# A streaming hybrid layer on one core: idle products in the norm gaps, a turn back through eight banks, a router that holds its weights, and queries projected last

## The chip, the cores and the metric

The kernel runs on one core of one Trainium2 chip. The metric is the device time in microseconds of one execution, from launch to end; lower is better. The profile is of one execution, and its span (first to last instruction) is a little shorter than its time. The engines are TensorE (PE in the rows; PEld is its weight load), VectorE (DVE), ScalarE (ACT), GpSimd (POOL) and SyncE (SP), which issues most transfers. L544 is line 544 of the kernel.

## The reference

One inference step of two layers, D = 1024, in float32, over 256 new prompt tokens and 32 sample tokens (T = 288 columns in all). Each layer:

```
z = x @ w_in, columns = [rnn stream | q | k | v | rnn gate | attn gate]
branch A: causal depthwise conv (width 4) -> RG-LRU (per-token linear recurrence)
branch B: rotary GQA over a chunk-banded sliding window with per-head sinks
m = sigmoid(g_rnn) * (A @ w_br_rnn) + sigmoid(g_attn) * (B @ w_br_attn)
x = LayerNorm(alpha * x + m @ w_out)
scores = sigmoid(x @ w_router); 8 of 64 experts by group-limited top-k of scores + e_bias
x = LayerNorm(alpha * x + shared_expert(x) + sum over the 8 of gate_e * expert_e(x))
```

There are 16 query heads and 2 key/value heads of 64; each expert is silu(x w1) * (x w3), then w2, with a hidden width of 256.

## The kernel before, in words

Activations stand feature-major in xT, eight chunks of 128 features by 288 tokens. The matrices of a layer, apart from the experts', are read in 33 pieces (PIECES) through a ring of three slots. SyncE asks for a piece when the piece three places earlier has been used. Work between engines is ordered by hand with semaphores.

**Projections.** over_features (L518) makes one chunk of output: eight products with a 128x128 weight and 288 moving columns; a float32 product shows as two records. The order is eight chunks of the recurrent stream, eight of Q, one of K, then V (L594). They go by turns into PSUM banks 0 and 1: item i uses bank i % 2, and bank_of waits until every earlier item of that bank has been evicted (z_free). ScalarE evicts the stream and V. VectorE runs the convolution (L1268, L1271), in layer 0 then decay_rates and sink_tables (small tables of parameters), and then the rotation of Q and K (L1287 to L1293), which reads the bank. The gate products of the recurrence (L602) follow, again by turns in banks 0 and 1, evicted by ScalarE with a sigmoid. Then come attention, the gates, the branch merge and w_out. VectorE's next work behind the last rotation is k_rows (L1297).

**Norms, two in each layer.** to_tokens turns the sum from feature-major to token-major: 24 turns (L552) into banks 2 to 7. VectorE takes statistics (L1226 and on), and ScalarE writes the normalised rows to tok (L936). When all are written, fill_xT turns them back (L544): for each of eight feature chunks, two turns of 128 rows and one of 32 into bank c % 2. ScalarE evicts the even chunks and VectorE the odd ones (norm_back, L944 and L1251), with gain and bias, into xT. TensorE waits at L544 for the rows, with nothing to do.

**Router, behind the first norm.** For each of three token tiles TensorE takes eight products with xT as stationary operand and 64 columns of w_router moving (L728); logits land token-major in bank 2. Then come shared_up(0) (16 products, L518), the rank products (L743 to L746) that wait for sel_ready, shared_up(1), and the first gather (L778 to L781). Meanwhile ScalarE rounds tok to a short format (xh, L1055) and VectorE makes the rest (xl, L1431), three tiles each. Then ScalarE takes the sigmoid of the logits (L1059), and VectorE runs the routing chain, L1441 to L1469 for the choice (sel_ready), to L1477 for the gate, then rank and the one-hot matrices.

**Experts.** A round is 16 turns of four experts, 15 of them in a hardware loop: up (L793), turn, down (L813), combine (L834, L835), gather. After the round TensorE loads the number of rounds from memory (L871), branches over the further rounds, which aren't needed here, and goes on to the second norm. The last layer ends with to_tokens(xT) and the store.

Of the kernel before, what the change touches and what calls it, by code (L numbers as in the profile page):

```python
# [53 lines left out]
SWAP = (0, 1, 5, 6)  # L54
QUAD = 4
# [24 lines left out]
Z_RNN, Z_Q, Z_K, Z_V, Z_LRU, Z_GATE, Z_OUT, Z_FILL1, Z_SH2, Z_FILL2, Z_N = 0, 8, 16, 17, 18, 34, 50, 58, 66, 74, 82  # L80
# [4 lines left out]
PIECES = ([("in", 256 * j) for j in range(4)] + [("q", j) for j in range(4)] + [("in", K_OFF)]  # L85
# [4 lines left out]
D_IN, D_Q, D_KV, D_G, D_BR, D_OUT, D_ROUTER = 0, 4, 8, 9, 17, 25, 29  # L90
# [25 lines left out]
def piece_landed(L, d):  # L116

    return L * SLOT_INC[d % RING] + sum(16 * DMAS.get(PIECES[x][0], 1) for x in range(d % RING, d + 1, RING))

# [6 lines left out]
def build(nc, inp, out, depth, alpha):  # L126
    with ExitStack() as ctx:
# [102 lines left out]
        s2.close()  # L230
        raw = B1f[:, 0:2 * depth * P].rearrange("p (k l c) -> p k l c", k=2, l=depth)
# [77 lines left out]
        xl_ready = sem("xl_ready")  # L309
        logits = sem("logits")  # L310
# [32 lines left out]
        def wait_piece_used(eng, L, d):  # L343

            kind, at = PIECES[d]
            if d < D_Q:
                i = Z_RNN + 2 * d + 1
            elif d < D_KV:
                i = Z_Q + 2 * (d - D_Q) + 1
            elif d == D_KV:  # L350
                i = Z_V
            elif d < D_BR:
# [4 lines left out]
            elif d < D_ROUTER:  # L357
                i = Z_OUT + 2 * (d - D_OUT) + 1
            elif kind == "router":
                eng.wait_ge(logits, L + 1)  # L360
# [145 lines left out]
        def _(pe):  # L506
            mm, transpose = nc.tensor.matmul, nc.tensor.transpose

            def bank_of(L, i):

                pe.wait_ge(z_free[i % 2], z_count(L, i))
                return ps[:, i % 2, :]
# [41 lines left out]

            for s in (w13_done, w2_done, c_full, ohT_full, hid_turned, xg_full):
                pe.sem_inc(s, FREE)
# [3 lines left out]
            fill_xT(lambda c: pe.wait_ge(z_free[c % 2], c // 2) if c >= 2 else None)  # L560
# [11 lines left out]
            for L in range(depth):  # L572
# [10 lines left out]
                for c in range(KC):  # L583
                    if c % 2 == 0:
                        piece(L, D_Q + c // 2)
                    over_features(bank_of(L, Z_Q + c), D_Q + c // 2, c % 2 * P, xk, T).then_inc(z_ready[c % 2], 1)

# [7 lines left out]
                last.then_inc(z_ready[Z_V % 2], 1)  # L595

# [119 lines left out]
                to_tokens(yP)  # L716
                pe.wait_ge(tok_act, (2 * L + 1) * NT)
# [150 lines left out]
                round_of(pe.snap(done), meanwhile=shared_down)  # L868
                pe.wait_ge(rounds_set, L + 1)
# [8 lines left out]
                to_tokens(ffT)  # L878
                pe.wait_ge(tok_act, (2 * L + 2) * NT)
# [10 lines left out]
        def _(act):  # L890
# [13 lines left out]
            def z_item(L, i):  # L904
                act.wait_ge(z_ready[i % 2], z_count(L, i) + 1)
                return ps[:, i % 2, :]
# [742 lines left out]
```

## Time and profile before

| | |
|---|---|
| time, median of 3 runs | 1719.76 us (1717.3 to 1720.46) |
| profiled execution, its own time | 1717.09 us |
| its span | 1715.3 us |
| TensorE busy | 1640.0 us, 96% |
| VectorE busy | 719.6 us, 42% |
| ScalarE busy | 495.4 us, 29% |
| mean granted TensorE clock | 0.972 of 2.4 GHz |

A granted clock of 1.00 is 2.4 GHz and 0.50 is 1.2 GHz. A row of instructions gives the start, the duration, engine, line, operation, output<-inputs, shape and count; in brackets the idle time of the engine just before, and what ended it. An engine that is not the bottleneck may idle at no cost.

### The profile page before, as it was taken

What the parts mean: (1) busy time and instruction counts of PE and PEld (TensorE: products, weight loads), DVE (VectorE), ACT (ScalarE), POOL (GpSimd) and SP (SyncE); (2) the same over time, 40 slices, a digit from 0 to 9 for tenths busy, and PEclk for the clock granted to TensorE, in tenths of its full rate; (3) what the DMA queues carried; (4) which work ended last, traced back from release to release, by engine and by line L of the source; (5) the groups of instructions that cost most, each with busy time, mean ns of one, the idle gap of its engine ahead of it and who ended that gap; (6) DMA issues with size and microseconds to landing.
All of it is one profiled execution on the core that took longest, in us unless ns stands there. A gap on an engine that the chain in (4) does not pass through costs nothing.

```text
span 1715.3 us, 24854 instructions
## 1 busy us (share of the span) xinstructions
PE 1640.0 (96%) x9230; PEld 1059.5 (62%) x9230; DVE 719.6 (42%) x1543; ACT 495.4 (29%) x1005; POOL 23.2 (1%) x38
## 2 busy tenths in 40 slices
PE   8999998999999999999799999989999999999995
PEld 5667897745545555555477779966555555545543
DVE  3646565333333323423445656562342333333323
ACT  1054434123223222232211544332223223223222
POOL 2000000000000000000010000000000000000000
PEclk9999997999999999999889999979999999999997
DMA  7644466299999999999246425554999999999960
GB/s 194 150 149 146 100 172 227 73 359 391 401 402 407 393 394 409 387 409 400 78 104 203 152 83 140 142 208 170 393 402 396 400 403 401 391 410 396 402 240 30
DMA packets 166339, 476.30 MB, mean 278 GB/s; under 512 B 43252, under 2 KB 99124, under 8 KB 133508
## 3 DMA queue, kind: packets, MB, share of 16 engines
q1 hardware_dynamic: 164480, 472.32, 73.5%
q0 software_dynamic: 1440, 2.98, 0.7%
q8 instruction: 42, 0.69, 0.2%
q14 instruction: 21, 0.17, 0.0%
q10 hardware_dynamic: 356, 0.13, 0.0%
HBM read 473.83 MB, written 1.57 MB: 277 GB/s over the span
## 4 chain that ended last, share of the span: by engine, by line
PE 94%; DVE 2%; ACT 2%; issue 1%; DMA 0%; POOL 0%; SPq 0%; DVEq 0%; ACTq 0%; POOLq 0%
PE ps L793 26%; PE ps L518 17%; PE ps L813 13%; PE ps L834 4%; PE ps L835 4%; PE ps L778 4%; PE ps L779 4%; PE ps L531 3%; PE ps L532 3%; PE ps L533 3%; PE ps L544 2%; PE ps L781 2%; PE ps L822 1%; PE ps L728 1%; DVE stats_of L1226 1%
## 5 line engine op out<-in xcount | busy, mean ns | idle before, releaser
L793 PE MATMUL ps<-experts,xg 128*64 128x512 f32 x2048 | 450.5, 592 | 2.8 <-ACT xg L1073 2.8
L793 PEld LDWEIGHTS ps<-experts,xg 128*64 128x64 f32 x2048 | 148.4, 137 | 293.0 <-issue 293.0
L518 PE MATMUL ps<-xT,dense 128*128 128x288 f32 x1184 | 302.7, 416 | 4.9 <-DVE tmp L1290 4.2
L518 PEld LDWEIGHTS ps<-xT,dense 128*128 128x128 f32 x1184 | 227.5, 194 | 70.3 <-issue 6.8
L813 PE MATMUL ps<-experts,hidT 128*64 128x512 f32 x1024 | 233.8, 598 | 1.8 <-ACT hidT L1087 1.8
L1507 DVE TENSOR_TENSOR hid<-ps,hid 128x256 f32<-128x256 f32 x64 | 27.2, 425 | 388.4 <-ACT hid L1081 388.4
L1095 ACT ACTIVATE yh<-ps,gsl 128x512 fp32r<-128x512 f32 x128 | 88.0, 687 | 228.2 <-PE ps L813 228.2
L1073 ACT ACTIVATE xg<-ps,gperm_all 128x256 f32<-128x256 f32 x256 | 130.6, 561 | 62.8 <-PE ps L781 59.2
L1519 DVE SCALAR_TENSOR_TENSOR yl<-ps,gsl,yh 128x512 fp32r<-128x512 f32 x128 | 96.1, 751 | 124.5 <-ACT yh L1095 124.5
L834 PE MATMUL ps<-ohT,yh 128*128 128x288 f32 x512 | 145.1, 308 | 3.1 <-DVE yl L1519 3.1
L813 PEld LDWEIGHTS ps<-experts,hidT 128*64 128x64 f32 x1024 | 68.5, 136 | 121.6 <-issue 121.6
L1081 ACT ACTIVATE hid<-ps 128x256 f32<-128x256 f32 x64 | 24.6, 384 | 400.5 <-PE ps L793 400.5
L835 PE MATMUL ps<-ohT,yl 128*128 128x288 f32 x512 | 139.9, 297 | 0.0
L778 PE MATMUL ps<-oh,xh 128*128 128x256 f32 x512 | 139.3, 294 | 0.0
L779 PE MATMUL ps<-oh,xl 128*128 128x256 f32 x512 | 133.2, 282 | 0.0
L1526 DVE TENSOR_TENSOR ffT<-ps,ffT 128x288 f32<-128x288 f32 x256 | 115.6, 457 | 24.8 <-PE ps L835 10.5
L834 PEld LDWEIGHTS ps<-ohT,yh 128*128 128x128 f32 x512 | 96.3, 188 | 29.2 <-issue 24.3
L531 PE MATMUL ps<-parts 128*128 128x288 f32 x384 | 113.5, 296 | 0.0
L533 PE MATMUL ps<-parts,dense_lo 128*128 128x288 f32 x384 | 112.9, 294 | 0.0
L778 PEld LDWEIGHTS ps<-oh,xh 128*128 128x128 f32 x512 | 97.6, 191 | 24.4 <-issue 24.3
L779 PEld LDWEIGHTS ps<-oh,xl 128*128 128x128 f32 x512 | 97.7, 191 | 0.1
L835 PEld LDWEIGHTS ps<-ohT,yl 128*128 128x128 f32 x512 | 96.4, 188 | 0.0
(253 smaller groups left out, 1707.6 us busy)
## 6 DMA issues: line engine op xcount, KB each, us to landing
experts<-in_w SPq DMA_DIRECT2D x384, 1024.0 KB, 9.5
dense<-in_w_in SPq DMA_DIRECT2D x26, 1024.0 KB, 5.4
dense<-in_w_in SPq DMA_DIRECT2D x32, 256.0 KB, 4.4
dense<-in_w_br_rnn SPq DMA_DIRECT2D x8, 1024.0 KB, 5.2
dense<-in_w_br_attn SPq DMA_DIRECT2D x16, 512.0 KB, 6.2
dense<-in_w_out SPq DMA_DIRECT2D x8, 1024.0 KB, 5.3
dense<-in_ws SPq DMA_DIRECT2D x6, 1024.0 KB, 5.6
tok<-in_x_prompt SPq DMA_DIRECT2D x1, 1024.0 KB, 5.3
```

What stands on the lines that cost most here:

```text
L518: last = mm(bank[:, 0:n], w[:, k, col:col + P], rhs(k), start=k == 0, stop=k == KC - 1)
L531: mm(bank[:, 0:T], w_hi[:, k, col:col + P], hi[:, k, :], start=k == 0, stop=False)
L533: last = mm(bank[:, 0:T], w_lo[:, k, col:col + P], hi[:, k, :], start=False, stop=k == KC - 1)
L778: mm(o, xh[:, t, x], oh[:, t, :], start=t == 0, stop=False)
L779: mm(o, xl[:, t, x], oh[:, t, :], start=False, stop=False)
L793: last = mm(ps[e % 2 * CAP:(e % 2 + 1) * CAP, 2, :], xg[:, k, e * CAP:e * CAP + CAP], experts[:, e, 0:2, k * DE:k * DE + DE], start=k == 0 ...
L813: last = mm(ps[e % 2 * CAP:(e % 2 + 1) * CAP, 3 + b, :], hidT[:, m, e % 2 * CAP:(e % 2 + 1) * CAP], experts[:, e, 2, m * D + b * 512:m * D ...
L834: mm(o, yh[:, u, c * P:c * P + P], ohT[:, u, :], start=u == 0, stop=False)
L835: last = mm(o, yl[:, u, c * P:c * P + P], ohT[:, u, :], start=False, stop=u == 1)
L1073: last = activation(xg[:, k, :], ps[:, SWAP[j], k % 2 * 256:k % 2 * 256 + 256], ACT.Identity, bias=gperm_all[:, L, 1, k:k + 1], scale=gper ...
L1519: V.scalar_tensor_tensor(yl[:, u, x], ps[:, 3 + b, :], gsl[:, u:u + 1], yh[:, u, x].bitcast(F32), ALU.mult, ALU.subtract).then_inc(yl_read ...
L1526: V.tensor_tensor(ffT[:, c, :], ps[:, SWAP[c % len(SWAP)], 0:T], ffT[:, c, :], ALU.add).then_inc(c_added, 1)
```

## The change

Four things change together.

1. Projections. K and V come before Q in items and pieces. Items 0 to 17 of a layer use six banks (i % 6), and an item waits only for the one six places earlier. VectorE rotates K first, then the queries, and runs decay_rates and sink_tables of layer 0 behind the last rotation.
2. Turning back. fill_xT puts its eight chunks into eight banks (FILL), with a wait ahead of the first two only. At the start of the program the parameter turns move to banks 6 and 7 and wait until xT is evicted.
3. Idle products. keep_clock multiplies the identity by 512 columns of constants, into a bank that nobody reads: six behind to_tokens of the first norm, three behind the round of experts, four behind to_tokens of the second norm.
4. Router. w_router is stationary (128x64) and xT moves, 288 columns, eight products into bank 0, each waiting only for its own chunk of xT. VectorE copies the transposed logits to lgT, TensorE turns them in three tiles into bank 2. The rounding of tok is spread: ScalarE does tiles 0 and 1 before the sigmoid and tile 2 after it; VectorE does tile 0, the copy of the logits, tile 1, the routing chain to the gate, and then tile 2.

```diff
+FILL = (0, 1, 4, 5, 6, 7, 2, 3)
-Z_RNN, Z_Q, Z_K, Z_V, Z_LRU, Z_GATE, Z_OUT, Z_FILL1, Z_SH2, Z_FILL2, Z_N = 0, 8, 16, 17, 18, 34, 50, 58, 66, 74, 82
+Z_RNN, Z_K, Z_V, Z_Q, Z_LRU, Z_GATE, Z_OUT, Z_FILL1, Z_SH2, Z_FILL2, Z_N = 0, 8, 9, 10, 18, 34, 50, 58, 66, 74, 82
+Z_DEEP = 6
-PIECES = ([("in", 256 * j) for j in range(4)] + [("q", j) for j in range(4)] + [("in", K_OFF)]
+PIECES = ([("in", 256 * j) for j in range(4)] + [("in", K_OFF)] + [("q", j) for j in range(4)]
...
+def z_bank(i):
+
+    return i % Z_DEEP if i < Z_LRU else i % 2
...
             def bank_of(L, i):
 
-                pe.wait_ge(z_free[i % 2], z_count(L, i))
-                return ps[:, i % 2, :]
+                if Z_DEEP <= i < Z_LRU:
+                    pe.wait_ge(z_free[i % 2], z_count(L, i - Z_DEEP) + 1)
+                elif i >= Z_LRU:
+                    pe.wait_ge(z_free[i % 2], z_count(L, i))
+                return ps[:, z_bank(i), :]
...
                 for c in range(KC):
-                    wait(c)
+                    if c < 2:
+                        wait(c)
                     for t, (at, n) in enumerate(TOK):
-                        last = transpose(ps[:, c % 2, at:at + n], tok[0:n, t, c * P:c * P + P], ident[0:n, 0:n])
+                        last = transpose(ps[:, FILL[c], at:at + n], tok[0:n, t, c * P:c * P + P], ident[0:n, 0:n])
...
+            def keep_clock(bank, n):
+
+                for _ in range(n):
+                    mm(ps[:, bank, :], ident, cst[:, 0:512], start=True, stop=True)
...
+            for b in range(2):
+                pe.wait_ge(z_free[b], Z_FIRST)
             for l in range(depth):
-                transpose(ps[:, 2, l * P:l * P + P], raw[:, 0, l, :], ident)
-                last = transpose(ps[:, 3, l * P:l * P + P], raw[:, 1, l, :], ident)
+                transpose(ps[:, 6, l * P:l * P + P], raw[:, 0, l, :], ident)
+                last = transpose(ps[:, 7, l * P:l * P + P], raw[:, 1, l, :], ident)
...
                 to_tokens(yP)
+                keep_clock(0, 6)
...
                 piece(L, D_ROUTER)
-                for b in range(2):
-                    pe.wait_ge(z_free[b], z_count(L, Z_FILL1 + KC))
                 w = dense[:, D_ROUTER % RING, 0:KC * NE].rearrange("p (k c) -> p k c", k=KC)
+                for k in range(KC):
+                    pe.wait_ge(z_free[k % 2], z_count(L, Z_FILL1 + k) + 1)
+                    last = mm(ps[0:NE, 0, 0:T], w[:, k, :], xT[:, k, :], start=k == 0, stop=k == KC - 1)
+                last.then_inc(logits_T, 1)
+                pe.wait_ge(logits_kept, L + 1)
                 for t, (at, n) in enumerate(TOK):
-                    for k in range(KC):
-                        last = mm(ps[0:n, 2, t * NE:t * NE + NE], xT[:, k, at:at + n], w[:, k, :], start=k == 0, stop=k == KC - 1)
+                    last = transpose(ps[0:n, 2, t * NE:t * NE + NE], lgT[0:NE, at:at + n], ident[0:NE, 0:NE])
                 last.then_inc(logits, 1)
...
                 round_of(pe.snap(done), meanwhile=shared_down)
+                keep_clock(2, 3)
                 pe.wait_ge(rounds_set, L + 1)
...
                 to_tokens(ffT)
+                keep_clock(0, 4)
...
-                if L == 0:
-                    decay_rates()
-                    sink_tables()
...
-                for c in range(KC + 1):
-                    i = Z_Q + c
-                    dst = qT[:, c, :] if c < KC else kT[:, :]
+                for c in range(-1, KC):
+                    i = Z_Q + c if c >= 0 else Z_K
+                    dst = qT[:, c, :] if c >= 0 else kT[:, :]
+                    if c == 0:
+                        dve.wait_ge(z_free[Z_V % 2], z_count(L, Z_V) + 1)
...
+                if L == 0:
+                    decay_rates()
+                    sink_tables()
...
+                keep_low(0)
+                dve.wait_ge(logits_T, L + 1)
+                V.tensor_copy(lgT[0:NE, :], ps[0:NE, 0, 0:T]).then_inc(logits_kept, 1)
+                keep_low(1)
...
                 V.scalar_tensor_tensor(gate[:, :, :], gate[:, :, :], ROUTED_SCALE, rb, ALU.mult, ALU.mult).then_inc(gate_ready, 1)
+                keep_low(2)
```

## Rows read from the trace of the kernel before

**Rows 1.** The page: TensorE's granted clock in 40 slices (tenths), and the final chain.

```profile
PEclk9999997999999999999889999979999999999997
...
PE 94%; DVE 2%; ACT 2%; issue 1%; DMA 0%; POOL 0%; SPq 0%; DVEq 0%; ACTq 0%; POOLq 0%
```

**Rows 2.** Table of stretches: length, busy PE, PEld, DVE, ACT, POOL, clock, DMA share, GB/s.

```profile
360.00:400.00 40.00, 40.00 (x226) 20.93 (x227) 13.85 (x25) 11.94 (x23) 0.00 (x0) 1.00 0.99 396
```

**Rows 3.** Waits: engine, line, releaser: us in total, times, longest.

```profile
PE ps L544 <- ACT tok L936: 23.1, 4, 6.3
```

**Rows 4.** Timeline of layer 0's projections, 43 to 64 us.

```profile
51.78 0.17 DVE L1175 TENSOR_SCALAR small<-small 128x16 f32<-128x16 f32 x1
...
58.46 0.46 DVE L1287 TENSOR_TENSOR qT<-ps,cst 128x288 f32<-128x288 f32 x1
...
60.93 3.53 PE L518 MATMUL ps<-xT,dense 128*128 128x288 f32 x7 [4.16 <-DVE tmp L1290]
```

**Rows 5.** Table of stretches about the clock, both layers (columns as in rows 2).

```profile
60.93:64.10 3.17, 3.17 (x7) 2.31 (x8) 3.05 (x7) 0.00 (x0) 0.00 (x0) 0.50 0.74 119
...
277.50:280.40 2.90, 2.81 (x24) 2.47 (x24) 1.98 (x5) 0.19 (x1) 0.00 (x0) 1.00 0.81 198
...
282.70:286.60 3.90, 0.00 (x0) 0.00 (x0) 3.30 (x11) 3.40 (x6) 0.00 (x0) 0.50 1.03 429
286.60:293.60 7.00, 6.95 (x24) 3.72 (x24) 1.99 (x4) 2.63 (x5) 0.00 (x0) 0.50 1.00 413
294.30:303.10 8.80, 8.77 (x48) 8.57 (x48) 5.93 (x5) 5.66 (x4) 0.00 (x0) 0.50 0.29 115
303.16:306.40 3.24, 3.24 (x8) 2.38 (x8) 2.39 (x28) 0.37 (x2) 0.00 (x0) 0.50 0.55 173
...
1144.20:1146.10 1.90, 1.90 (x5) 1.47 (x5) 1.28 (x15) 0.37 (x2) 0.00 (x0) 0.50 0.44 37
...
1700.60:1705.90 5.30, 5.29 (x24) 4.44 (x24) 2.06 (x3) 1.19 (x2) 0.00 (x0) 0.50 0.00 0
```

**Rows 6.** Timeline of layer 0's last rotation and first gate products, 86 to 110 us.

```profile
89.76 5.60 PE L594 MATMUL ps<-dense,xT 128*128 128x128 f32 x48
...
90.51 1.85 DVE L1290 TENSOR_TENSOR tmp<-ps,cst 32x288 f32<-32x288 f32 x4
...
97.89 1.22 PE L602 MATMUL ps<-B,wax 128*128 128x291 f32 x4 [1.15 <-ACT B L965]
...
107.92 0.29 DVE L1297 COPY k_rows<-ps 128x128 f32<-128x128 f32 x1 [15.07 <-PE ps L623]
```

**Rows 7.** Timeline, first norm to the first gather: layer 0, then layer 1.

```profile
286.61 6.95 PE L544 MATMUL ps<-cst,tok 128*128 128x128 f32 x24 [6.26 <-ACT tok L936]
...
295.19 3.77 DVE L1431 TENSOR_TENSOR xl<-tok,xh 128x1024 fp32r<-128x1024 f32 x2 [1.01 <-ACT xh L1055]
...
303.67 0.36 DVE L1441 TENSOR_TENSOR rt<-score,ebias_all 128x192 f32<-128x192 f32 x1 [2.48 <-ACT score L1060]
...
310.81 0.36 DVE L1469 TENSOR_TENSOR sel<-rt,cst 128x192 f32<-128x192 f32 x1
...
314.62 7.98 PE L518 MATMUL ps<-xT,dense 128*128 128x288 f32 x32
...
322.22 0.49 PE L778 MATMUL ps<-oh,xh 128*128 128x256 f32 x1
...
1127.61 6.95 PE L544 MATMUL ps<-cst,tok 128*128 128x128 f32 x24 [6.26 <-ACT tok L936]
...
1162.57 0.50 PE L778 MATMUL ps<-oh,xh 128*128 128x256 f32 x1
```

**Rows 8.** Load of the round count (line view), then the timeline behind it.

```profile
L871 PEldq TENSOR_LOAD <-rounds x2: 312/400/487, 839.1 to 1679.5; - x2
...
843.78 1.32 PE L552 MATMUL ps<-cst,ffT 128*128 128x128 f32 x5 [3.35 <-issue]
...
846.86 4.32 PE L552 MATMUL ps<-cst,ffT 128*128 128x128 f32 x19 [1.76 <-issue]
```

More of the change, by code:

```diff
@@ L89 @@
 ND = len(PIECES)
-D_IN, D_Q, D_KV, D_G, D_BR, D_OUT, D_ROUTER = 0, 4, 8, 9, 17, 25, 29
+D_IN, D_KV, D_Q, D_G, D_BR, D_OUT, D_ROUTER = 0, 4, 5, 9, 17, 25, 29
 RING = 3
@@ L230, in build @@
         s2.close()
+        lgT = ffT[:, 0, :]
         raw = B1f[:, 0:2 * depth * P].rearrange("p (k l c) -> p k l c", k=2, l=depth)
@@ L309, in build @@
         xl_ready = sem("xl_ready")
+        logits_T = sem("logits_T")
+        logits_kept = sem("logits_kept")
         logits = sem("logits")
@@ L345, in wait_piece_used @@
             kind, at = PIECES[d]
-            if d < D_Q:
+            if d < D_KV:
                 i = Z_RNN + 2 * d + 1
-            elif d < D_KV:
-                i = Z_Q + 2 * (d - D_Q) + 1
             elif d == D_KV:
                 i = Z_V
+            elif d < D_G:
+                i = Z_Q + 2 * (d - D_Q) + 1
             elif d < D_BR:
@@ L359, in wait_piece_used @@
             elif kind == "router":
-                eng.wait_ge(logits, L + 1)
+                eng.wait_ge(logits_T, L + 1)
                 return
@@ L581, in _ @@
                     over_features(bank_of(L, Z_RNN + m), D_IN + m // 2, m % 2 * P, xk, T).then_inc(z_ready[m % 2], 1)
[L583 to L586, printed above, removed]
                 piece(L, D_KV)
@@ L595, in _ @@
                 last.then_inc(z_ready[Z_V % 2], 1)
+                for c in range(KC):
+                    if c % 2 == 0:
+                        piece(L, D_Q + c // 2)
+                    over_features(bank_of(L, Z_Q + c), D_Q + c // 2, c % 2 * P, xk, T).then_inc(z_ready[c % 2], 1)
                 pe.wait_ge(wax_in, (L + 1) * 64)
@@ L942, in norm_back @@
                 for c in range(0, KC, 2):
-                    bank = z_item(L, first + c)
+                    act.wait_ge(z_ready[0], z_count(L, first + c) + 1)
+                    bank = ps[:, FILL[c], :]
                     activation(xT[:, c, :], bank[:, 0:T], ACT.Identity, bias=prm_all[:, L, b * KC + c:b * KC + c + 1],
@@ L1050, in _, with keep_high @@
                 norm_back(L, V_G1, V_B1, Z_FILL1)
-                for t, (at, n) in enumerate(TOK):
-                    act.wait_ge(tok_act, (2 * L) * NT + (t + 1))
-                    if t == NT - 1:
-                        act.wait_ge(tok_dve, 2 * L + 1)
+                def keep_high(t):
+                    n = TOK[t][1]
                     activation(xh[0:n, t, :].rearrange("p (k f) -> p f k", k=KC),
                                tok[0:n, t, :].rearrange("p (f k) -> p f k", k=KC), ACT.Copy).then_inc(xh_ready, 1)
+                act.wait_ge(tok_act, (2 * L + 1) * NT)
+                act.wait_ge(tok_dve, 2 * L + 1)
+                keep_high(0)
+                keep_high(1)
                 act.wait_ge(logits, L + 1)
@@ L1249, in norm_back @@
                 for c in range(1, KC, 2):
-                    bank = z_item(L, first + c)
+                    dve.wait_ge(z_ready[1], z_count(L, first + c) + 1)
+                    bank = ps[:, FILL[c], :]
                     V.tensor_scalar(xT[:, c, :], bank[:, 0:T], prm_all[:, L, g * KC + c:g * KC + c + 1],
@@ L1426, in _, with keep_low @@
                 norm_back(L, V_G1, V_B1, Z_FILL1)
-                for t, (at, n) in enumerate(TOK):
+                def keep_low(t):
+                    n = TOK[t][1]
                     dve.wait_ge(xh_ready, L * NT + t + 1)
```

17 lines of the change are left out of this document (9 added, 8 removed).

## The prediction

> **What bounds the kernel now.** I read the page first: what busies TensorE, and at what clock. TensorE makes 94% of the chain that ended last, and its granted clock is full but for four short dips [rows 1]. The table of stretches then says which stages can give anything. In the expert loop TensorE is busy 40.00 of 40 us at full clock, and the loads, at 396 GB/s, keep up [rows 2]: nothing in the change touches this loop, and what is won ahead of it is kept. What is left are the gaps between such stages. The waits of TensorE name the largest: it waits four times, 23.1 us in all, for ScalarE's normalised rows [rows 3]; the change doesn't shorten these waits, it fills them.
>
> The projections of layer 0 have a second gap: VectorE spends 51.78 to 58.46 on decay_rates and sink_tables, only then rotates the first query chunk, and TensorE, with two banks, stands 4.16 us [rows 4].
>
> Last, the clock. It is low in 60.93 to 64.1, after that gap, and then rises under dense products. After the first norm's turn to tokens (24 turns in 2.81 us at full clock) TensorE idles and the clock is 0.50; it stays there through the turn back (24 turns, 6.95 us) and through the 64-column router products (8.8 us), and rises only some 3.2 us after shared_up(0) began (1.9 us in layer 1) [rows 5]. The reader is to see that turns back do not bring it up, though the row calls the engine busy, while dense products do within 1.9 to 3.3 us.
>
> **The change, part by part.**
>
> Projections. K and V go ahead of Q, six banks, and decay_rates and sink_tables go behind the last rotation. Layer 0 loses the 4.16 us stand and 3.2 us at half clock, worth 1.6: 5.8 us [rows 4, 5]. The moved 6.65 us of VectorE work begin when the last query chunk is rotated; VectorE had 15.07 us idle at that place before k_rows [rows 6], about 10 us after the change, so it is hidden with some 3 us over. The matrices are read in another order from the same three slots, each asked for as early before its use as now, and TensorE waits for no piece today: nothing. Ahead of the recurrence gates TensorE now waits for VectorE to free the last query chunk. Before, V ended at 95.3 and the second pair of gate products began 2.6 us later, held by ScalarE (whose table load is now early). After, the second product needs the rotation's last read, 90.51 + 1.85 = 92.36 against a chunk that ended at 89.76: 2.65, and then one product of 0.6, so 3.25 [rows 6]: 0.65 us lost in each layer. At the start, four parameter turns that ran beside the last evictions of xT now come behind them, 4 x 0.22 = 0.9 at most [rows 5]; I take 0.65, once. Sum for the projections: 5.8 - 3 x 0.65 = 3.8 us won. More banks alone give layer 1 nothing: the one stand on a projection bank among TensorE's waits is that of layer 0.
>
> First norm, both layers. From the first turn back (286.61) to the first gather product (322.22) are 35.6 us, in layer 1 35.0 [rows 7]. I rebuild that stretch.
> - Idle products. Six of 512 columns behind to_tokens. A product of 288 columns costs 0.485 (16 in 7.8 us, [rows 7]), so 0.86 each at full clock, 5.2 of the 6.26 us gap: they end 1.1 us before the rows do and delay nothing.
> - The turn back. It costs 6.95 / 8 = 0.87 us a chunk with TensorE busy throughout, so no bank holds it and eight banks alone give nothing. How long it takes at full clock no row shows. Bounds: 6.95 as now, and 2.8 by the 24 turns to tokens at full clock. At half clock a plain turn takes 5.3 / 24 = 0.22 [rows 5]; a chunk has the columns of 2.25 such, 0.50, and the other 0.37 I put down to the change between 128 and 32 rows, as fixed. Then a chunk at full clock takes 0.25 + 0.37 = 0.62, eight 5.0. Whether the clock stays is the open question. The engine is fed sparsely here: the same turns never raised it. I take it that it falls within them: 6.0.
> - The router. Eight products of 288 columns instead of 24 pairs of 64: 3.9 us at full clock. They are dense, so the clock comes back under them as under every dense run: 1.9 to 3.3 us at half, costing 1.5. Taken 5.4 against 8.8.
> - What is new behind it. Logits are copied by VectorE (0.46, by the 288-column evictions), turned by TensorE, and go to the sigmoid: about 1.9 in all, but VectorE does keep_low(1) after the copy, 1.9 us [rows 7], and two small copies, 0.25, so the routing chain begins 0.1 + 0.46 + 1.9 + 0.25 = 2.7 after the router. keep_low(0) is done by then: of the row of two from 295.19 it is the first half, and ends 3.5 after the turn back. The chain takes 303.67 to 311.17, 7.5 us [rows 7]. Behind sel_ready stand the rank products (2.0 with the wait's end, 0.1) and shared_up(1), 314.62 to 322.22, 7.6 us. Shared_up(0), 7.8 us at full clock, begins 1.1 after the router and is done 1.3 before sel: it costs nothing, and TensorE waits 1.3 there. keep_low(2), another 1.9, sits between gate and rank: VectorE is ready for the gather 6.7 after sel, TensorE at 9.7; nothing, and 3.0 us of cover.
> Sum: 6.0 + 5.4 + 2.7 + 7.5 + 2.1 + 7.6 = 31.3. Won: 4.3 and 3.7, together 8.0. With the clock full throughout, 5.0 + 3.9 instead: 28.8, together 13.0. With no help from the fill and a late rise (6.95 + 5.7): 32.5, together 5.6.
>
> Second norm. The three products behind round_of stand ahead of the load of the round count. That load ran at 839.1, while TensorE worked on until 843.78 - 3.35 = 840.43: the queue runs on beside the array, so these products (2.6 us) lie inside the stand until 843.78; their dispatch costs perhaps 0.3 in each layer [rows 8]. Behind them stands a second pause of 1.76 us after five turns, in layer 0 only, for which no engine is named; it may move with the code, 1.8 either way. The four products behind to_tokens take 3.4 at full clock and 6.8 at half; from 846.86 + 4.32 = 851.2 that would end at 858.0; of the 23.1 us of waiting [rows 3] three gaps of 6.26 leave 4.3 for this one, so the rows are ready at 855.5 and up to 2.5 is lost. I take 0.4. The turn back may save 0.95 in each layer as above. The final turn to tokens, 5.3 us at half clock [rows 5], would take less at full clock; I count nothing. Sum: 1.9 - 0.6 - 0.4 = 0.9 won.
>
> The Trainium skill, TensorE: Matmul & The Clock Gate, section "What's actually happening", says that the gate follows how busy the engine has recently been. The trace agrees in kind (the clock falls in every norm gap). By that rule alone a filled gap keeps its clock, which is the rival B below; but the same rule asks whether sparse turns count as busy, and that speaks against this change's reach.
>
> **The sum.** 3.8 + 8.0 + 0.9 = 12.7 us off the profiled execution, 1717.1 to 1704.4 (span 1715.3). That execution is 2.7 below the median of the three runs, 1719.8; on the median the forecast is 1707.
>
> **Rivals.**
> A, as above: projections 3.8, the clock falls in the turns back and returns under the router: 1707; 0.55.
> B, the clock holds through the norms: projections 3.8, first norm 13.0, second 8.0 (2.0 in each turn back, 1.5 in layer 1's first products if they spend 3 us at half clock as others do, 2.5 in the last turn to tokens): 24.8, so 1695. For it: dense idle products end only 1.1 us before the turn back. Against it: in the last gap 23.1 / 4 - 3.4 leaves over 2 us idle, and sparse turns follow. 0.20.
> C, the norms give less than their refill costs: the clock falls as before, the turn back stays 6.95, the late rise costs more, the four products overrun in both layers by 2: 3.8 + 5.6 - 2.9 = 6.5, 1713; 0.17.
> D, no change to be seen: the array is slow when the six products start. They then take 10.3 against 6.26, 4.0 lost in each first norm, and with C's terms 3.8 + 5.6 - 2.9 - 8.0 = -1.5: 1721. It needs the clock low at 280, where the row shows it full. 0.05.
> E, slower: the added instructions shift the code of the expert loop, and a pause such as the 1.76 us one [rows 8] appears once in each turn: 15 turns and 2 layers, 30 x 1.76 = 53, less 12.7: 1760. It decides from 0.5 us a turn. Against it: the loop has no stand at all now. 0.03.
> The Trainium skill, Runtime: NRT & Kernel Launch, section "Instruction fetch mechanics", says that a taken branch to a distant page stalls the engine; the pause behind the round count fits, none in the loop does.
>
> **How the numbers follow.** Less than 0.2%, 3.4 us, can't be told from no change. A, B and C are faster: 0.92; D is the same: 0.05; E slower: 0.03. The time is A's, 1707. The range goes from 1697, into B and its open size, to 1714, past C; outside are the far part of B (0.08) and D and E.
>
> **What would show it.** Projections: no stand of TensorE near 57 and no dip behind it; gate products begin some 5 us earlier in layer 0. Norm: 26 idle products of 512 columns (6 + 3 + 4 in each layer), the granted clock 1.00 until the turn back begins; whether it is 1.00 or 0.50 within the turn back decides A against B. From the turn back to the gather 31.3 us. The forecast fails if the routing chain isn't what releases the ranks, if to_tokens starts later behind the round count, or if the expert loop shows a stand.

## The result, and the profile after

The change makes the kernel faster: 1695.63 us median of 4 runs (1692.05 to 1698.02) against 1720.03 (1717.30 to 1720.46), ratio 0.9866, 95% interval 0.9853 to 0.9878. The forecast was 1707, with 1697 as its lower end: right in sign, 11 us too slow. The profiled executions have spans of 1715.3 and 1692.4 us, so 22.9 us are to be found. All ratios are of fast executions; one of the six of three_products below took 5750 us at a granted clock of 0.283 and counts in no ratio.

The page of the kernel after, its row of granted clock and its final chain, against [rows 1]:

```profile
PEclk9999999999999999999999999999999999999998
...
PE 94%; DVE 3%; ACT 1%; issue 1%; DMA 0%; POOL 0%; SPq 0%; DVEq 0%; ACTq 0%; POOLq 0%
```

Three of the four dips are gone at this resolution. The timeline of TensorE in layer 0's projections and gate products, against [rows 4] and [rows 6] (the wait before a row stands in brackets):

```profile
15.70 0.44 PE L585 MATMUL ps<-cst,B 128*128 128x128 f32 x1 [0.64 <-DVE xT L1189]
...
59.39 31.31 PE L531 MATMUL ps<-xT,dense 128*128 128x288 f32 x128
90.54 0.65 PE L623 MATMUL ps<-B,wax 128*128 128x291 f32 x2
93.19 10.23 PE L623 MATMUL ps<-B,wax 128*128 128x291 f32 x30 [2.00 <-DVE tmp L1321]
```

The stand of 4.16 us is gone; a wait of 0.64 at the start and one of 2.00 for the last rotation are new. The tables, now behind it, are hidden: the copy of k_rows still idles 3.43 us (it was 15.07). The first norm, idle products to the first gather, layer 0 and then layer 1, against [rows 7]:

```profile
275.99 5.32 PE L572 MATMUL ps<-cst 128*128 128x512 f32 x12
...
282.42 5.92 PE L558 MATMUL ps<-cst,tok 128*128 128x128 f32 x24 [1.11 <-ACT tok L962]
288.27 5.43 PE L748 MATMUL ps<-xT,dense 128*64 128x288 f32 x16
...
303.62 0.43 PE L768 MATMUL ps<-sel,cst 128*128 128x64 f32 x2 [1.03 <-DVE sel L1508]
...
313.28 0.50 PE L802 MATMUL ps<-oh,xh 128*128 128x256 f32 x1
...
1106.38 5.32 PE L572 MATMUL ps<-cst 128*128 128x512 f32 x12
1112.80 4.42 PE L558 MATMUL ps<-cst,tok 128*128 128x128 f32 x24 [1.10 <-ACT tok L962]
1117.15 4.09 PE L748 MATMUL ps<-xT,dense 128*64 128x288 f32 x16
...
1140.48 0.49 PE L802 MATMUL ps<-oh,xh 128*128 128x256 f32 x1
```

One code, the same wait of 1.1 us ahead of it, and two durations. The table of stretches, with the columns of [rows 2], says why:

```profile
275.90:281.31 5.41, 5.41 (x15) 2.19 (x12) 4.84 (x16) 3.09 (x7) 0.00 (x0) 1.00 1.05 415
281.31:282.42 1.11, 0.00 (x0) 0.00 (x1) 0.84 (x3) 1.06 (x2) 0.00 (x0) 1.00 1.01 421
282.42:284.20 1.78, 1.78 (x10) 1.15 (x11) 0.82 (x2) 0.64 (x2) 0.00 (x0) 0.99 1.04 433
284.20:288.30 4.10, 4.10 (x16) 2.13 (x15) 1.15 (x2) 1.92 (x4) 0.00 (x0) 0.50 0.99 410
288.30:291.00 2.70, 2.70 (x7) 1.41 (x7) 1.59 (x2) 2.70 (x2) 0.00 (x0) 0.50 1.03 411
291.00:293.70 2.70, 2.70 (x11) 1.23 (x9) 0.92 (x1) 1.99 (x2) 0.00 (x0) 1.00 0.58 229
1112.80:1117.20 4.40, 4.40 (x25) 2.73 (x25) 1.98 (x4) 2.26 (x4) 0.00 (x0) 1.00 1.02 423
1117.20:1121.20 4.00, 4.00 (x17) 2.06 (x16) 2.52 (x2) 3.98 (x4) 0.00 (x0) 1.00 1.01 406
```

The clock column (third from the right) is full through the idle products and the wait. In layer 0 it falls 1.8 us into the turn back, with TensorE busy all along, and is back 2.7 us into the router's products; in layer 1 it holds. So case A happened in layer 0 and case B in layer 1. The second norm of layer 0, the kernel before (its rows behind [rows 8]) and then the kernel after:

```profile
855.54 6.95 PE L544 MATMUL ps<-cst,tok 128*128 128x128 f32 x24 [4.36 <-ACT tok L936]
863.21 67.72 PE L518 MATMUL ps<-xT,dense 128*128 128x288 f32 x272 [0.72 <-DVE xT L1251]
```

```profile
831.33 2.74 PE L572 MATMUL ps<-cst 128*128 128x512 f32 x6
835.02 2.07 PE L566 MATMUL ps<-cst,ffT 128*128 128x128 f32 x17 [0.95 <-issue]
838.11 0.94 PE L566 MATMUL ps<-cst,ffT 128*32 128x128 f32 x7 [1.01 <-issue]
838.88 3.60 PE L572 MATMUL ps<-cst 128*128 128x512 f32 x8
844.12 4.41 PE L558 MATMUL ps<-cst,tok 128*128 128x128 f32 x24 [1.64 <-ACT tok L962]
849.25 35.16 PE L531 MATMUL ps<-xT,dense 128*128 128x288 f32 x144 [0.72 <-ACT xT L971]
```

From the turn to tokens to the turn back it was 855.54 - 843.78 = 11.76 us and is 9.10; from there to layer 1's first product 7.67 and 5.13.

The ledger, from differences between the same events of the two traces (gains are positive):

| stretch | forecast | measured |
|---|---|---|
| start to layer 0's first norm | 5.8 - 2 x 0.65 = 4.5 | 286.61 - 282.42 = 4.2 |
| first norm, layer 0: 35.61 to 30.86 | 4.3 | 4.75 |
| expert loop to the second turn to tokens | -0.3 | -0.2 |
| second norm of layer 0: 11.76 + 7.67 to 9.10 + 5.13 | 0.55 | 5.2 |
| layer 1's products up to its first norm | -0.65 | 264.40 - 263.55 = 0.85 |
| first norm, layer 1: 34.96 to 27.68 | 3.7 | 7.3 |
| from there to the end | 0.65 | 0.8 |
| sum | 12.7 | 22.9 |

The gate products, from the first of them to the turn of kT behind the last, take 12.14 us in the kernel before and 12.71 in the kernel after, in both layers: the wait of 2.00 us costs 0.57 a layer, near the 0.65 forecast. So the 0.85 won in layer 1 leaves 1.4 for the clock at the layer's start, less this 0.57: the kernel before had 0.50 there (863 to 865 us), the kernel after 1.00.

### The profile page after: what moved, and what is told of

It reads as the page before. It is cut to its first block, busy times and chain, and to the rows that moved or that the text cites. A ratio compares the mean times of both kernels' runs of the same rounds, so it can differ in the third digit from the quotient of the medians.

```text
span 1692.4 us, 24839 instructions
## 1 busy us (share of the span) xinstructions
PE 1640.8 (97%) x9224; PEld 1047.6 (62%) x9224; DVE 719.6 (43%) x1545; ACT 496.6 (29%) x1005; POOL 23.2 (1%) x38
## 4 chain that ended last, share of the span: by engine, by line
PE 94%; DVE 3%; ACT 1%; issue 1%; DMA 0%; POOL 0%; SPq 0%; DVEq 0%; ACTq 0%; POOLq 0%
PE ps L817 26%; PE ps L531 16%; PE ps L837 14%; PE ps L858 4%; PE ps L859 4%; PE ps L802 4%; PE ps L803 4%; PE ps L544 3%; PE ps L545 3%; PE ps L546 3%; PE ps L805 2%; PE ps L558 2%; PE ps L846 1%; PE ps L623 1%; DVE stats_of L1257 1%; PE ps L782 1%
## 5 line engine op out<-in xcount | busy, mean ns | idle before, releaser
L531 PE MATMUL ps<-xT,dense 128*128 128x288 f32 x1184 | 297.6, 411 | 0.7 <-ACT xT L971 0.7
L531 PEld LDWEIGHTS ps<-xT,dense 128*128 128x128 f32 x1184 | 223.9, 191 | 63.9 <-issue 1.4
```

Of the source, the lines that this page charges most:

```text
L531: last = mm(bank[:, 0:n], w[:, k, col:col + P], rhs(k), start=k == 0, stop=k == KC - 1)
```

## Experiments

Theory 1: idle products that reach close to the turn back keep the clock through it, and this is most of what the norms won. Theory 2: the dense router and the eight banks did it and the products nothing. All ratios are against the kernel before on the same chip (its medians 1717.7 to 1718.6 us); one thousandth is 1.7 us. The kernel after stands at 0.9866 (0.9853 to 0.9878). A trace is of one execution of its kernel.

| run | median, us | ratio | 95% interval |
|---|---|---|---|
| no_products | 1709.17 | 0.9943 | 0.9930 to 0.9957 |
| no_products_first | 1707.52 | 0.9940 | 0.9927 to 0.9954 |
| three_products | 1707.02 | 0.9933 | 0.9921 to 0.9946 |
| no_load_products | 1697.69 | 0.9881 | 0.9866 to 0.9896 |
| more_products | 1691.57 | 0.9839 | 0.9826 to 0.9853 |
| between_chunks | 1701.01 | 0.9894 | 0.9877 to 0.9912 |
| products_only | 1712.11 | 0.9961 | 0.9948 to 0.9975 |
| old_router | 1703.74 | 0.9913 | 0.9899 to 0.9926 |
| two_banks | 1698.00 | 0.9883 | 0.9868 to 0.9898 |
| projections_only | 1713.44 | 0.9972 | 0.9961 to 0.9984 |
| tables_after | 1711.29 | 0.9963 | 0.9949 to 0.9977 |
| queries_first | 1695.58 | 0.9865 | 0.9851 to 0.9879 |
| queries_first_more | 1688.88 | 0.9826 | 0.9813 to 0.9839 |
| last_seven | 1688.50 | 0.9827 | 0.9814 to 0.9840 |
| start_wait | 1686.64 | 0.9821 | 0.9807 to 0.9834 |

**Without the products.** The kernel after with all three calls out:

```diff
-                keep_clock(0, 6)
...
-                keep_clock(2, 3)
...
-                keep_clock(0, 4)
```

> The kernel after without one of its idle products (all three keep_clock calls left out); eight-bank turn back, new router, projections kept. Theory 1 (the products keep the granted clock full until the turn back starts, and this is most of what the norms won): the clock is at its lower level when the first turn back starts, the stretch from the first turn back to the first gather is about 34 us in layer 0 and 33 in layer 1 instead of 30.9 and 27.7, the second norm's turn back takes 6 to 9 us instead of 4.4, and the time is about 1708 us, 10 to 15 above the kernel after. Theory 2 (the dense router and the eight banks do it, the products nothing): within 2 us of the kernel after, about 1696.

Timeline of TensorE in its first norm of layer 0 and its second norm:

```profile
282.86 6.95 PE L558 MATMUL ps<-cst,tok 128*128 128x128 f32 x24 [6.26 <-ACT tok L959]
289.74 6.54 PE L747 MATMUL ps<-xT,dense 128*64 128x288 f32 x16
...
839.22 2.83 PE L566 MATMUL ps<-cst,ffT 128*128 128x128 f32 x24 [3.49 <-issue]
848.31 6.95 PE L558 MATMUL ps<-cst,tok 128*128 128x128 f32 x24 [6.25 <-ACT tok L959]
```

Theory 1 holds: (0.9943 - 0.9866) x 1718.6 = 13 us are the products', and all four turns back take 6.95 us again. Not all of the 13 us lie in the norms: see the gate products of the next run. The row of 839.22 shows something else: its 24 turns run unbroken, as fast as at full clock, and the turn back starts 9.09 us after them, as in the kernel after. So 2.7 of the 5.2 us in layer 0's second norm need no product. They are the pause of 1.76 us in the kernel before and the slow turns behind it [rows 8], and they went without any product there.

**Only the second norms' products.** One line out, the one in the first norm:

```diff
-                keep_clock(0, 6)
```

> The kernel after without the 6 idle products of the first norms; the 3 and 4 of the second norms stay. Theory 1 (each set of products earns in its own norm): it loses what the first norms' products earn, 2.5 to 3.5 us in layer 0, where the clock of the kernel after fell inside the turn back, and 5 to 6 in layer 1, where it held: 1703 to 1705. Rival (the second norms' products earn nearly all, the first norms' gain is the router and the banks): within 3 us of the kernel after.

The expectation was 1703 to 1705, and neither theory holds: the loss is nearly the whole 13 us; the second norms' seven products alone are worth nothing that can be told (0.9940 against 0.9943). The first norms' stretches are 34.4 and 32.5 us. Another 4.3 us are lost from layer 1's first product to its first norm (852.88 to 1111.63, against 849.25 to 1103.73), where no product was taken out. Timeline and stretches of that run:

```profile
927.61 0.65 PE L623 MATMUL ps<-B,wax 128*128 128x291 f32 x2
930.26 1.38 PE L623 MATMUL ps<-B,wax 128*128 128x291 f32 x3 [2.00 <-DVE tmp L1320]
```

```profile
927.00:930.20 3.20, 1.26 (x6) 0.64 (x4) 2.27 (x5) 0.50 (x1) 0.00 (x0) 1.00 0.30 70
930.20:934.00 3.80, 3.74 (x9) 2.15 (x10) 0.46 (x2) 1.51 (x3) 0.00 (x0) 0.57 1.09 406
```

The clock falls behind the wait of 2.00 us that the new projection order brought in, and it started the layer low (0.54 over 848 to 858 us). In the kernel after neither happened, at the same instructions and the same wait. The fall at that wait shows in layer 1 of five of the ten profiles with the new order (this one, no_products, three_products, old_router, between_chunks), whose gate products then take 13.9 to 14.0 us instead of 12.71. It shows in layer 0 of none, and in none of the seven profiles with queries ahead of K and V, where the wait is 1.15 us. So 1.3 of the 13 us that no_products lost lie there. What decides between the five and the other five no run shows.

**Half of the products.** 3, 1 and 2 for 6, 3 and 4:

```diff
-                keep_clock(0, 6)
+                keep_clock(0, 3)
```

> The kernel after with half of its idle products: 3, 1 and 2 instead of 6, 3 and 4. Theory 1 (what counts is the idle time left between the last product and the turn back): about 3.8 us of wait are left ahead of each turn back, the clock is at its lower level there, and most of the gain of the products is gone: 1703 to 1709. Rival (any products in the gap are enough to keep the clock): within 2 us of the kernel after.

Stretches of its first norm (products, wait, turn back):

```profile
276.50:279.10 2.60, 2.60 (x7) 0.85 (x5) 2.36 (x7) 0.86 (x3) 0.00 (x0) 1.00 1.07 405
279.15:282.80 3.65, 0.00 (x0) 0.00 (x0) 3.06 (x10) 3.17 (x6) 0.00 (x0) 1.00 1.00 420
282.85:288.75 5.90, 5.90 (x25) 3.30 (x25) 1.95 (x4) 2.54 (x5) 0.00 (x0) 0.64 1.00 416
```

The time is as Theory 1 said, but the clock is not: it is still full through 3.65 us of waiting and falls inside the turn back. A full clock at the start of the turns is not enough.

**More products.** 7 for 6 and, behind the second turn to tokens, 6 for 4:

```diff
-                keep_clock(0, 6)
+                keep_clock(0, 7)
...
-                keep_clock(0, 4)
+                keep_clock(0, 6)
```

> The kernel after with 7 idle products instead of 6 after the first norm's turn to tokens and 6 instead of 4 after the second's. In the kernel after TensorE still waited 1.1 us for the norm after the 6 products, and 1.6 and 2.8 us after the 4. Theory 1 (what the products buy is a clock that is still full when the turn back starts and is not lowered inside it, so less idle time ahead of it helps): the products fit into the wait at 0.9 us each, cost nothing, and the clock falls in fewer of the four turn backs: 1 to 4 us faster than the kernel after, about 1693. Rival (the clock falls through the turn back's own transposes, whatever came before): within 1 us of the kernel after, or up to 2 us slower from products that end later than the norm.

4.6 us faster than the kernel after, with intervals that just touch at 0.9853. The wait ahead of the first turns back is down to 0.25 us, and the turns back of three norms are at full clock, 4.41 us each; the fourth still takes 5.40. Stretches of those three and of the fourth:

```profile
281.80:286.10 4.30, 4.30 (x24) 2.64 (x24) 1.94 (x4) 2.19 (x4) 0.00 (x0) 1.00 1.02 423
841.30:845.60 4.30, 4.30 (x25) 2.63 (x24) 1.73 (x3) 2.21 (x4) 0.00 (x0) 1.00 0.02 4
1111.70:1116.00 4.30, 4.30 (x25) 2.63 (x25) 1.89 (x4) 2.25 (x4) 0.00 (x0) 1.00 1.00 417
1670.10:1675.40 5.30, 5.30 (x24) 3.01 (x24) 1.73 (x3) 2.36 (x4) 0.00 (x0) 0.74 0.01 3
```

All profiles of kernels with the eight-bank turn back (but for between_chunks) say the same of the wait just ahead of it. With 0.25 us or none it took 4.4 us in 14 cases of 14 (more_products and the three fastest kernels). With 1.1 to 1.8 us it took 4.4 in 6 of 14 and 5.4 to 6.4 in the others. With 2.8 us and more it never took less than 5.6, in 16 cases.

**Products inside the turn back.**

```diff
+                    if busy and c in (2, 5):
+                        mm(ps[:, FILL[c], :], ident, cst[:, 0:512], start=True, stop=True)
```

> The kernel after with one more idle product ahead of the third and one ahead of the sixth chunk of every turn back but the first. Each costs 0.9 us on the path at full clock (0.44 a record, two records), 1.8 a turn back, 7.1 in all. Theory 1 (the clock falls in a turn back because of its short transposes with waits between them; the kernel after lost 3 us in layer 0's first norm and 3.5 in the last norm to it): the clock holds in all four, the two losses of 3 to 3.5 us go, and the time is within 2 us of the kernel after, from 1695 to 1698. Rival (the fall comes from the idle time ahead of the turn back, so products inside come too late): 5 to 7 us slower than the kernel after, about 1701.

In three norms the clock held (no stretch from the first norms is slower than 29.8 us, against 27.7 to 28.1 for a held clock without these products), but each pair costs 1.8 us on the path. In the last norm, with 2.82 us of wait ahead, it fell in spite of them, and it fell at layer 1's gate products. The time came out as the rival's, 1701.0 (single executions from 1696.8 to 1704.8), by another way in three norms: not too late, but too dear.

**Without the three products at the load.**

```diff
-                keep_clock(2, 3)
```

> The kernel after without the 3 idle products ahead of the load of the round count; the 6 and 4 stay. Theory 1 (the 3 products lie wholly in the pause of 3.4 us ahead of the second turn to tokens, and the clock is anyway full for most of it, but enters the norm's wait after a longer idle stretch): the turn to tokens starts at the same distance from the last combine or 0.2 us earlier, the clock falls in one or both second norms, 1 to 4 us slower than the kernel after. Rival (they only cost their dispatch): up to 0.5 us faster.

0.9881 against 0.9866, intervals overlapping: not settled by times. In the trace, of its fastest execution (1694.51 us), TensorE stands 3.20 us ahead of the second turn to tokens, which then takes 4.19 us instead of 2.8, and the turn back behind it 5.47. In the same trace both first norms hold their clock (28.05 and 27.82 us), with the code of the kernel after.

**The products alone, in the kernel before.**

```diff
                 to_tokens(yP)
+                keep_clock(0, 6)
```

and so at the other two places.

> The kernel before with the idle products alone (6 after the first norm's turn to tokens, 3 and 4 at the second's); two-bank turn back, old router, old projections. Theory 1: the products alone win most of the second norms and a part of the first: turn backs at full clock at their start, a gain of 8 to 13 us, about 1709. Theory 2: nothing or a loss of up to 2 us, since the old router, which TensorE runs at about 8 us or more at full clock too, has few columns an instruction and lets the clock fall again.

0.9961, 6.7 us: a gain, but below the 8 to 13 of Theory 1. The turns back take 5.8 and 5.9 us in the first norms, but the old router follows. Stretches of the two in layer 0:

```profile
287.50:293.10 5.60, 5.32 (x24) 2.98 (x24) 1.89 (x4) 2.50 (x5) 0.00 (x0) 0.77 1.01 418
294.00:302.80 8.80, 8.80 (x49) 8.51 (x49) 5.92 (x5) 5.61 (x4) 0.00 (x0) 0.50 0.42 166
```

**The old router in the kernel after.**

```diff
...
-                for k in range(KC):
-                    pe.wait_ge(z_free[k % 2], z_count(L, Z_FILL1 + k) + 1)
-                    last = mm(ps[0:NE, 0, 0:T], w[:, k, :], xT[:, k, :], start=k == 0, stop=k == KC - 1)
...
+                for t, (at, n) in enumerate(TOK):
+                    for k in range(KC):
+                        last = mm(ps[0:n, 2, t * NE:t * NE + NE], xT[:, k, at:at + n], w[:, k, :], start=k == 0, stop=k == KC - 1)
...
```

> The kernel after with the router as it was (24 products of 64 columns whose weights are the tokens, straight into the logits; no transposes of logits, no copy by VectorE). Theory 1 (each of the 24 products loads weights of up to 128 columns for 64 columns of work): the router takes 7 to 9 us instead of 4.1 to 5.4, so each layer is 3 to 5 us longer and the time about 1702. Theory 2 (the new router is only a gain because the clock was low in the kernel before): at the clock held by the products the old router is no longer than the new with its copy and turn, within 1.5 us of the kernel after.

8 us slower than the kernel after, as Theory 1 said. The trace is of its slowest execution (1708.11 us). In layer 0 the router takes 8.9 us with the clock at 0.50; in layer 1, where the turn back kept its clock (4.41 us), it takes 6.56: the clock is 1.00 for its first 2.2 us and then falls (0.59 over the next 2.0). The new one took 5.43 and 4.09. The products and the rest of the change earn more together than apart: the products alone 6.7 us, all the rest alone 9.8, both 23. The router is part of that: put in with the products it earns these 8 us.

**Two banks for the turn back.**

```diff
-FILL = (0, 1, 4, 5, 6, 7, 2, 3)
+FILL = (0, 1, 0, 1, 0, 1, 0, 1)
...
-                    if c < 2:
-                        wait(c)
+                    wait(c)
...
```

The start's own turn back gets such waits too, and the logits move to bank 4.

> The kernel after with its turn back through two banks, as before (a wait on the copy of the chunk two earlier; the router's logits in bank 4). Theory 1 (a chunk takes TensorE 0.54 us at full clock, a copy out by ScalarE or VectorE with its wait about the same as two chunks): the two-bank turn back takes about 5.5 us instead of 4.4 at full clock, twice a layer, so 3 to 5 us slower than the kernel after, about 1700, and more where the slack lets the clock fall earlier. Rival (the banks are worth nothing, since two chunks cover one copy): within 1 us of the kernel after.

2.9 us slower, with intervals that overlap by 0.001. The trace shows what the time leaves open. The stretch of its second turn back in layer 0, and one of its weight loads (timeline of PEld):

```profile
842.40:847.50 5.10, 4.61 (x24) 2.67 (x24) 1.73 (x3) 2.31 (x4) 0.00 (x0) 1.00 0.01 3
...
845.01 0.20 PEld L557 LDWEIGHTS ps<-cst,tok 128*128 128x128 f32 x2 [0.25 <-ACT xT L970]
```

At full clock TensorE is busy 4.61 of 5.10 us; the turn back takes 5.03 us, 0.6 more than the 4.41 of the kernel after. It waits three times, 0.25 us each, for ScalarE's eviction of a bank (the load of 845.01 is one).

**The projection part alone, and the tables alone.** The first is the kernel after with two-bank turn back, old router and no products. The second is the kernel before with

```diff
-                if L == 0:
-                    decay_rates()
-                    sink_tables()
...
                     dve.wait_ge(q_ready, L * (KC + 1) + c + 1)
+                if L == 0:
+                    decay_rates()
+                    sink_tables()
```

> The kernel after with the projection part alone: K and V before the queries, six banks, decay_rates and sink_tables last; two-bank turn back, old router, no idle products (the split order of the router's high and low parts is kept too). Theory 1 (the ledger of the two profiled runs: the first event past the projections is 4.2 us earlier than before in layer 0 and nothing further in layer 1): about 4 us faster than before, 1714.5. Rival (part of the 4.2 us comes from elsewhere, or the norms' order adds 2 us a layer): outside 1712.5 to 1716.5.

> The kernel before with one edit: decay_rates and sink_tables after the rotary loop instead of before it. Theory 1 (in the kernel before VectorE reached the first query's bank late because of these two, and TensorE waited 4.2 us for it in layer 0): this alone wins most of the projection part, 3 to 4.2 us, about 1715. Rival (order and six banks are what wins): under 1.5 us, since the rotary of two-bank chunks stays slower than TensorE, and the key's rows come no sooner.

4.8 and 6.4 us: the two moved calls alone give the whole gain of the part, and the time doesn't tell the rest from nothing. In the traces, from the first turn of the program to the first norm's turn to tokens, the kernel before takes 277.54 - 8.02 = 269.52 us, the tables alone 270.94 - 8.16 = 262.78, the whole part 272.70 - 7.43 = 265.27. So the order and the six banks cost 2.5 us there: 0.68 at the start and 0.57 at the gate products are told above, the remaining 1.2 are not explained. With the tables alone no wait for a projection bank is left, and layer 0's gate products wait 1.15 us, as in the kernel before, not 2.00; timeline of that run:

```profile
83.17 5.60 PE L594 MATMUL ps<-dense,xT 128*128 128x128 f32 x48
88.70 1.45 PE L602 MATMUL ps<-B,wax 128*128 128x291 f32 x4
91.30 1.22 PE L602 MATMUL ps<-B,wax 128*128 128x291 f32 x4 [1.15 <-ACT B L965]
```

**The old order in the kernel after, then with more products.** Queries ahead of K and V, two banks, tables still last.

```diff
-Z_RNN, Z_K, Z_V, Z_Q, Z_LRU, Z_GATE, Z_OUT, Z_FILL1, Z_SH2, Z_FILL2, Z_N = 0, 8, 9, 10, 18, 34, 50, 58, 66, 74, 82
-Z_DEEP = 6
+Z_RNN, Z_Q, Z_K, Z_V, Z_LRU, Z_GATE, Z_OUT, Z_FILL1, Z_SH2, Z_FILL2, Z_N = 0, 8, 16, 17, 18, 34, 50, 58, 66, 74, 82
+Z_DEEP = 2
...
```

The pieces and the loops of TensorE and VectorE follow the order.

> The kernel after with the projections in the order of the kernel before (queries, then K and V, two banks), and only decay_rates and sink_tables moved behind the rotary loop. Theory 1 (read from the run with the tables moved alone: its first pair of scores at 100.8 us against 103.3 in the kernel after; with the queries last, TensorE's second gate product waits 2.0 us for VectorE's last rotary, and there are no K and V products to cover it): 2 to 3 us faster than the kernel after, about 1693. Rival (the order is neutral, the difference of the two runs is from elsewhere): within 1 us of the kernel after.

> As the run before it, with 7 idle products in the first norms and 6 in the second. Theory 1 (the two edits are independent: minus 4 for the products, minus 2.5 for the order): about 1689, the fastest so far. Rival (they share a gain through where the clock falls): no better than the better of the two, 1691.5.

The first shows no gain, so the 2 to 3 us expected did not come. Its trace, of its slowest execution (1699.62 us), has the clock falling in all four turns back (5.4, 6.4, 5.75 and 6.4 us), which hides what the shorter wait at the gate products gives, 0.57 us a layer. The second is at 1689 as expected, 0.0013 below more_products with overlapping intervals, so its time doesn't show that the order earns anything. Where the clock is full at the start of layer 1, the way from there to the first norm's turn to tokens takes 253.8 us (this run) against 254.5 (the kernel after).

**Seven in the last norm, and the start.** The edit is against the run before:

```diff
-                keep_clock(0, 6)
+                keep_clock(0, 6 + L)
```

> As the run before it, with 7 instead of 6 idle products in the first and second... in both norms of layer 1 where the number was 6 (the second norm), layer 0 as it was. In the run with more products the last turn back still had a wait of 1.1 us ahead and took 5.4 us instead of 4.4, and the turn to tokens behind it 4.4 instead of 2.8. Theory 1 (less idle time ahead keeps the clock): 0.5 to 2.5 us faster than the run before it. Rival (the last norm's fall does not come from the wait ahead): within 0.7 us.

The same time (0.9827 against 0.9826), as the rival said, but not for its reason. The expectation read the slow last turn back in more_products; in the profile of queries_first_more that turn back already took 4.41 us, so only the final turn to tokens (4.25 us, now 2.81) was left to gain. The turn to tokens ahead was slow in this execution, 4.46 us behind a pause of 2.28. Then, on top:

```diff
-                pe.wait_ge(z_free[b], Z_FIRST)
+                pe.wait_ge(z_free[b], 3)
```

> The run with the old projection order and 7, 6 and 7 idle products, with one more edit: the start's transposes of the parameter rows wait only until banks 6 and 7 are copied out (three copies an engine, not four). The kernel after waits 0.64 us there, the kernel before did not. Theory 1: most of the 0.64 us comes back, about 0.5 us faster than without the edit (1688.5), inside what a run can tell; the trace shows the wait gone and the first projection product 0.5 us sooner behind the first turn. Rival: the wait moves to the projections' own wait for the last two copies, and the first product stays where it was.

The wait is gone: first projection product 15.82 - 8.06 = 7.76 us behind the first turn, against 16.57 - 8.13 = 8.44. The time is 1 us lower, within the intervals. This is the fastest kernel measured, 0.9821, 31 us below the kernel before (its interval overlaps those of the two runs ahead of it); its clock row and its last two groups of TensorE:

```profile
PEclk9999999999999999999999999999999999999999
```

```profile
1666.88 4.41 PE L558 MATMUL ps<-cst,tok 128*128 128x128 f32 x24 [0.25 <-ACT tok L962]
1672.05 2.81 PE L566 MATMUL ps<-cst,xT 128*128 128x128 f32 x24 [0.76 <-DVE xT L1283]
```

## Why the prediction was wrong, step by step

- **The step that failed** is the choice "I take it that it falls within them: 6.0", made for every turn back. It held in layer 0's first norm (5.92) and in layer 1's second (5.68), and failed in the other two: layer 1's first (4.42) and layer 0's second (4.41). It makes 3.6 us in layer 1's first norm (the router behind it kept its clock too), 1.6 in layer 0's second, and 1.5 in the products behind that one (0.85 against -0.65), which the forecast gave to case B alone: 6.7 of the 10.2 us between forecast and measured. The runs show in its place that the products decide it by how near the turn back they end: 14 of 14 turns back kept the clock with 0.25 us of wait or none, 6 of 14 with 1.1 to 1.8, none with 2.8 and more. The Trainium skill, TensorE: Matmul & The Clock Gate, section "What's actually happening", ties the gate to how busy the engine has lately been; the runs agree in kind, since 0, 3, 6 and 7 products in each first norm (and 0, 3, 7 and 9 in each second) give 0.9943, 0.9933, 0.9866 and 0.9839.
- **The fixed pause.** "It may move with the code, 1.8 either way" was priced at nothing in the sum. This is the second failed term. It moved: the stretch to layer 0's turn back fell from 11.76 to 9.10 us, 2.7 us won, and in no_products as well. What is left of it (1.01 us) lies inside ScalarE's work and costs nothing. It needs no product to go; projections_only, tables_after and the kernel before have it (11.5 to 12.0 us), and the kernels with the new router or with products don't have it at that size. Why, no run shows.
- **Turn back at full clock**: 5.0 forecast from half-clock rows, 4.4 measured. The fixed part of a chunk was too large: 0.37 us taken, where 0.87 and 0.55 a chunk at the two clocks leave 0.23. Router: 3.9 and 4.09 at full clock, 5.4 and 5.43 with the fall. The rebuilt stretch: 31.3 against 30.86 with the fall, 28.8 against 27.7 to 28.1 without. The chain behind the router was right: the wait for sel 1.3 against 1.03, keep_low(2) hidden.
- **"Eight banks alone give nothing"** is right at half clock and wrong at full clock, where two banks cost 0.6 us in the one turn back that shows it.
- **Projections**: 4.5 against 4.2 in layer 0. The 0.65 us at the start was 0.64 of wait, and the gate products behaved as worked out (93.19 - 90.54 = 2.65 to the second product, 0.57 lost against 0.65). Which edit earns the gain was not asked: the move of the tables does, and the traces show the new order and the six banks only as a cost, which the times can't resolve.
- **Second norm's products**: hidden as said. The loss of 0.4 us for the four did not come; they end 1.64 us before the rows.
- **Rivals.** C, D and E did not occur. B's 1695 is the number that came, but partly by luck: in the profiled execution the clock held in two norms of four, and 2.7 us are the pause, which B did not count. The fastest kernel, which holds the clock in all four and has the old order besides, is at 1686.64. The chance of 0.20 for B treated the four norms as one event; had each norm been priced apart, with two of them held, the forecast would have stood half way between A and B, at 1701.

Open: what decides, at the same code and the same wait of 1.1 us, whether the clock falls in a turn back. It fell in layer 0 and held in layer 1 of one execution, and held in both of no_load_products. Also open is what sets the pause behind the round count.

## What to carry to other kernels

Fill a gap on TensorE nearly to its end (here to 0.25 us) ahead of a stretch of small transposes, not merely partly: half of the products gave almost nothing, and one more in each first norm and two more in each second gave 4.6 us. Look also at what stays on TensorE behind the gap: here the 24 products of 64 columns lost in layer 1 the clock that had been kept, so price the two as a pair. Test each piece of a change alone: here two moved calls carried a reorder and four more banks that cost 2.5 us up to the first norm, and its wait of 2 us is one more place where the clock fell, in five profiles of ten.

## What was not expected of the hardware

- The granted clock fell from 1.00 to 0.50 while TensorE was busy 100% of the stretch with small transposes (284.20:288.30 above), 1.78 us behind a wait of 1.11.
- It stayed at 1.00 through a wait of 3.65 us behind 2.6 us of products (three_products), and fell only in the turns behind it.
- A pause for which no engine is named broke the second turn to tokens after 5 or 6 records for 1.76 to 2.6 us (kernel before, tables_after, projections_only), after 13 to 17 for 0.85 to 1.5 (the kernel after and seven more, queries_first and more_products among them), or not at all (no_products, old_router and four more). In layer 1 the same code never showed it.
